# Two transformer blocks in one kernel: another order of block two's input chunks, later rotations in block one, one selection product, and one early Exp

## The reference, cut to what matters

```python
u = _rmsnorm(h, norm_mix)
p = _split_columns(u @ w_in)          # q_a k_a v_a | q_b k_b v_b q_idx k_idx w_idx | q_c k_cmp v_cmp k_sel v_sel k_win v_win g_c | g_merge
o_a = _stick_breaking(q_a, k_a, v_a)                    # log_sigmoid and exp of scores
o_b = _dsa_attention(_rope(q_b), rope1(k_b), v_b, _rope(q_idx), rope1(k_idx), w_idx)      # top 64 keys
o_c = _nsa_attention(_rope(q_c), rope1(k_cmp), v_cmp, rope1(k_sel), v_sel, rope1(k_win), v_win, gates, ...)
merged = g[0] * (o_a @ w_up[0]) + g[1] * (o_b @ w_up[1]) + g[2] * (o_c @ w_up[2])
```

## Time and profile before

| | us |
|---|---|
| median of 3 runs | 909.33 |
| lowest, highest of them | 908.6, 909.56 |
| the profiled execution, its own time | 909.91 |
| its span, first to last instruction | 907.4 |
| PE busy in the span | 882.2 |
| DVE, ACT, POOL busy | 606.8, 480.5, 29.2 |

### The profile page before, as it was taken

The page is one execution under the profiler, slowest core; times in us unless marked ns, Lnnn a source line. Parts: engine busy times, 40 slices in busy tenths (PEclk is TensorE's granted clock), DMA queues, the critical chain, the costliest instruction groups (busy, mean ns, idle before and its releaser), DMA issues.

```text
span 907.4 us, 15435 instructions
## 1 busy us (share of the span) xinstructions
PE 882.2 (97%) x6552; PEld 748.8 (83%) x6552; DVE 606.8 (67%) x976; ACT 480.5 (53%) x775; POOL 29.2 (3%) x51
## 2 busy tenths in 40 slices
PE   7999999999899999999999999999999999999997
PEld 4999898787689888888889978776788788888885
DVE  4578978557856666656766577877863566666673
ACT  4775667436534444456444856484622545555561
POOL 0010000010000000000000020000000000000000
PEclk9999999999999999999999999999999999999999
DMA  9644333224468665555339764353817566665521
GB/s 336 190 140 140 99 119 114 63 83 150 178 248 282 188 190 190 200 202 187 121 112 229 164 210 144 111 186 107 277 38 206 146 187 188 191 193 194 199 95 47
DMA packets 131204, 150.71 MB, mean 166 GB/s; under 512 B 11808, under 2 KB 102176, under 8 KB 131008
## 3 DMA queue, kind: packets, MB, share of 16 engines
q1 hardware_dynamic: 129920, 145.57, 51.8%
q10 hardware_dynamic: 1216, 4.16, 1.2%
HBM read 148.67 MB, written 1.05 MB: 165 GB/s over the span
## 4 chain that ended last, share of the span: by engine, by line
PE 85%; DVE 7%; ACT 4%; issue 2%; DMA 1%; POOL 0%; POOLq 0%; ACTq 0%; DVEq 0%
PE psum L821 12%; PE psum L716 9%; PE psum L718 9%; PE psum L717 9%; PE psum L826 7%; PE psum L774 4%; PE psum L794 3%; PE psum L795 3%; PE psum L803 3%; PE psum L722 3%; PE psum L870 2%; PE psum L880 2%; PE psum L871 2%; PE psum L827 2%; DVE parts L2705 2%
## 5 line engine op out<-in xcount | busy, mean ns | idle before, releaser
L1808 ACT ACTIVATE parts<-low 128x1024 fp32r<-128x1024 f32 (+3 forms) x252 | 254.3, 1044 | 65.6 <-PE psum L718 48.3
L2705 DVE TENSOR_TENSOR parts<-low,parts 128x1024 fp32r<-128x1024 f32 (+3 forms) x156 | 183.7, 1206 | 37.7 <-ACT parts L1808 37.5
L716 PE MATMUL psum<-parts 128*128 128x512 f32 (+2 forms) x424 | 169.1, 399 | 4.6 <-DVE parts L2705 2.5
L718 PE MATMUL psum<-parts 128*128 128x512 f32 (+2 forms) x424 | 163.5, 386 | 0.0
L717 PE MATMUL psum<-parts 128*128 128x512 f32 (+2 forms) x424 | 163.4, 385 | 0.0
L1808 ACT ACTIVATE high<-psum 128x512 f32<-128x512 f32 (+6 forms) x115 | 63.4, 560 | 134.2 <-PE psum L827 76.4
L821 PE MATMUL psum<-parts 128*128 128x512 f32 x462 | 116.8, 392 | 0.0
L716 PEld LDWEIGHTS psum<-parts 128*128 128x128 f32 x424 | 79.6, 188 | 26.3 <-DVE parts L2705 4.5
L821 PEld LDWEIGHTS psum<-parts 128*128 128x128 f32 x462 | 86.9, 188 | 16.9
L718 PEld LDWEIGHTS psum<-parts 128*128 128x128 f32 x424 | 79.6, 188 | 16.4
L717 PEld LDWEIGHTS psum<-parts 128*128 128x128 f32 x424 | 79.8, 188 | 13.9
(11 more groups left out here) (313 smaller groups left out, 1310.6 us busy)
## 6 DMA issues: line engine op xcount, KB each, us to landing
low<-in_w_in_dram SPq DMA_DIRECT2D x40, 1024.0 KB, 5.3
low<-in_w_ffn_in_dram SPq DMA_DIRECT2D x44, 512.0 KB, 5.2
low<-in_w_ff_in_dram SPq DMA_DIRECT2D x16, 1024.0 KB, 5.7
low<-in_w_ff_out_dram SPq DMA_DIRECT2D x16, 1024.0 KB, 4.8
low<-in_w_ffn_out_dram SPq DMA_DIRECT2D x11, 1024.0 KB, 5.0
low<-in_w_out_dram SPq DMA_DIRECT2D x8, 1024.0 KB, 5.2
low<-in_w_ple_gate_dram SPq DMA_DIRECT2D x4, 1024.0 KB, 5.0
low<-consts_dram ACTq DMA_DIRECT2D x1, 2078.0 KB, 9.0
```

The source lines that it names most:

```text
L716: mm(o, l[0], r[0], start, False)
L718: return mm(o, l[1], r[0], False, stop)
L1808: return e.activation(o, a, ACT.Copy)
L2705: tt(rslot3(n, nk, width)[:, r, 0:w], slot3(n, nk, width)[:, r, 0:w], st.hi3(j)[:, r, 0:w].bitcast(F32), ALU.subtract) \
```

## The change

It has five parts.

1. The order of `plan_2` is now: q_b, q_idx, the four keys, the narrow k_cmp with v_cmp, q_c. `rope_to` and the numbers in the waits follow. The function `ahead` goes, so every split stands in its place ahead of the wait for the chunk. The copies of keys on ACT move from the end of the last chunk into `read_vt`. The values' `token_range` uses banks 5 and 6.
2. Block one's rotations are done later (`turned_at`), with four buffers `rt1`.
3. The sum over four groups of partitions is one matmul for each head, against a new constant, `C_SEL`.
4. ACT does one Exp of one column after `main_b`.
5. The constants grow by 128 columns (from 2078 KB by 64 KB).

```diff
-C_END = C_SINC + 256
+C_SEL = C_SINC + 256
+C_END = C_SEL + 128
+    c[:, C_SEL:C_SEL + 16] = r % 32 == s[:, 0:16]
...
-        rt1 = [view3(P + 9216 + 1024 * i, 2, 256) for i in range(2)]
+        rt1 = [view3(P + 8704 + 512 * i, 2, 256) for i in range(4)]
...
-            return RC[:, 6:10:3, :] if n == 5 else RC[:, 10:11, :] if n == 6 else RC[:, 2 * (n - 2):2 * (n - 2) + 2, :]
+            return RC[:, 6:10:3, :] if n == 4 else RC[:, 10:11, :] if n == 5 else RC[:, 4:6, :] if n == 6 else RC[:, 2 * (n - 2):2 * (n - 2) + 2, :]
...
         plan_2 = [([(0, 256, 0)], [128, 128]), ([(256, 256, 0)], [128, 128]), ([(768, 256, 0)], [128, 128]),
-                  ([(1152, 256, 0)], [128, 128]), ([(1476, 256, 0)], [128, 128]),
-                  ([(1024, 64, 0), (1408, 64, 64), (1860, 64, 128), (1988, 64, 192)], [128, 128]), ([(1732, 128, 0)], [128])]
+                  ([(1152, 256, 0)], [128, 128]), ([(1024, 64, 0), (1408, 64, 64), (1860, 64, 128), (1988, 64, 192)], [128, 128]),
+                  ([(1732, 128, 0)], [128]), ([(1476, 256, 0)], [128, 128])]
...
-                yield from token_range(st2, 5, 2, 464, lambda i: [main_act.at("vt2", i), main_dve.at("vt2", i)], nothing)
+                yield from token_range(st2, 5, 2, 464, lambda i: [main_act.at("vt2", i), main_dve.at("vt2", i)], nothing, (5, 6))
...
-                    for g in range(4):
-                        t = mm(p[:, 16 * h:16 * h + 16], hd[:, h, :], ident[:, 32 * g:32 * g + 16], g == 0, g == 3)
+                    t = mm(p[:, 16 * h:16 * h + 16], hd[:, h, :], const(C_SEL, 16), True, True)
...
-            def ahead(st, j):
-                return st.tag == "st2" and j == 5
             def feature_chunk(st, j, widths, read):
                 steps = 1 + len(widths)
                 for n in range(steps):
-                    if n == 1 or n == 0 and not ahead(st, j + 1):
+                    if n < 2:
                         split(st, j + 1, (n,))
                     yield
                 q.wait_ge(*main_pe.at(st.tag, j, 1))
-                if ahead(st, j + 2):
-                    split(st, j + 2, (0,))
                 read()
...
-                if n >= (2 if tag == "qk" else 4):
-                    q.wait_ge(*rope_dve.at(tag, n - 2))
+                if n >= 4:
+                    q.wait_ge(*rope_dve.at(tag, n - (4 if tag == "qk" else 2)))
...
             def read_vt(i, p):
+                if i == 0:
+                    q.wait_ge(*rope_dve.at("in2", 4))
+                    for m, half in enumerate(half_rows[::-1]):
+                        copy(RC[half, 7, :], RC[half_rows[1], 6, :]).then_inc(key_act.up(m), 1)
+                    q.wait_ge(*key_act.at(1))
+                    copy(RC[half_rows[1], 6, :], RC[half_rows[0], 6, :]).then_inc(key_act.up(2), 1)
                 copy(vt[:, i, 0:256], p[:, 0:256])
...
             turns.alone(main_b())
+            act(first_exp, ident[:, 0:1], ACT.Exp).then_inc(stick_act.up("table"), 1)
...
+            turned_at = ((), (), (0,), (1,), (2, 3), (4,))
...
-                    yield from feature_chunk(st1, QK_AT + n, [128, 128], (lambda n=n: rope1(n - 1)) if n else nothing, nothing)
+                    yield from feature_chunk(st1, QK_AT + n, [128, 128], lambda n=n: [rope1(m) for m in turned_at[n]], nothing)
```

More of the change, by code:

```diff
@@ L351, in program @@
         sm_nsa = [(small(4), small(4), small(4), small(4)) for _ in range(2)]
+        first_exp = small(1)
         sm_mem = [(small(4), small(4), small(4)) for _ in range(2)]
@@ L833, in wide_chunk, with token_range @@
                 yield
-            def token_range(st, j0, n, w, freed, late):
+            def token_range(st, j0, n, w, freed, late, banks=None):
                 nk = 8 // n
-                banks = [next(pg), next(pg)]
+                banks = banks or [next(pg), next(pg)]
                 for s in range(n):
@@ L1541, in scores @@
                     bank(b)
-                q.wait_ge(*rope_dve.at("in2", 5))
+                q.wait_ge(*rope_dve.at("in2", 6))
                 q.wait_ge(*key_act.at(2))
@@ L1626, in nsa @@
                     bank(b)
-                q.wait_ge(*rope_dve.at("in2", 4))
+                q.wait_ge(*rope_dve.at("in2", 6))
                 q.wait_ge(*cmp_act.at("kc"))
@@ L1884, in feature_chunk, with token_range @@
                 q.wait_ge(*main_pe.at(st.tag, j, 1))
-                if ahead(st, j + 2):
-                    split(st, j + 2, (0,))
                 read()
                 yield
-            def token_range(st, j0, n, read):
+            def token_range(st, j0, n, read, banks=None):
                 nk = 8 // n
-                banks = [next(pg), next(pg)]
+                banks = banks or [next(pg), next(pg)]
                 for s in range(n):
@@ L1895, in token_range @@
                         for r in range(nk // 2):
-                            if i == 0 and (r == 1 or r == 0 and not ahead(st, j0 + s + 1)):
+                            if i == 0 and r < 2:
                                 split(st, j0 + s + 1, (r,))
@@ L2000, in qkv @@
                     b = next(pg)
-                    yield from feature_chunk(st1, QK_AT + n, [128, 128], lambda: rope_read("qk", n, 2, b, rt1[n % 2], qk[:, 2 * n:2 * n + 2, :]))
+                    yield from feature_chunk(st1, QK_AT + n, [128, 128], lambda: rope_read("qk", n, 2, b, rt1[n % 4], qk[:, 2 * n:2 * n + 2, :]))
             def gate(r):
@@ L2363, in read2 @@
                 else:
-                    m = 1 if n == 6 else 2
+                    m = 1 if n == 5 else 2
                     rope_read("in2", n, m, b, rz2[n % 2][:, 0:m, :], rope_to(n))
@@ L2376, in main_b @@
                     yield from feature_chunk(st2, n - 2, plan_2[n][1], lambda: read2(n, b))
[L2377 to L2383, removed]
+                yield from token_range(st2, 5, 2, read_vt, (5, 6))
             turns.alone(main_b())
+            act(first_exp, ident[:, 0:1], ACT.Exp).then_inc(stick_act.up("table"), 1)
             pa2 = itertools.cycle((2, 3, 4))
@@ L2742, in feature_chunk, with token_range @@
                 yield
-            def token_range(st, j0, n, read, late):
+            def token_range(st, j0, n, read, late, banks=None):
                 nk = 8 // n
-                banks = [next(pg), next(pg)]
+                banks = banks or [next(pg), next(pg)]
                 for s in range(n):
@@ L3291, in rope2 @@
                 if n >= 2:
-                    m = 1 if n == 6 else 2
-                    rope("in2", n, m, rz2[n % 2][:, 0:m, :], rope_to(n), *((C_COSC, C_SINC) if n == 6 else (C_COS, C_SIN)))
+                    m = 1 if n == 5 else 2
+                    rope("in2", n, m, rz2[n % 2][:, 0:m, :], rope_to(n), *((C_COSC, C_SINC) if n == 5 else (C_COS, C_SIN)))
             def read_vt(i, p):
                 if i == 0:
-                    q.wait_ge(*rope_dve.at("in2", 5))
+                    q.wait_ge(*rope_dve.at("in2", 4))
                     for m, half in enumerate(half_rows):
@@ L3310, in main_b @@
                     yield from feature_chunk(st2, n - 2, plan_2[n][1], lambda: rope2(n - 1), nothing)
-                yield from token_range(st2, 5, 2, read_vt, lambda: rope2(6))
+                yield from token_range(st2, 5, 2, read_vt, lambda: rope2(6), (5, 6))
             turns.alone(main_b())
@@ L3834, in nsa_keys @@
                 e.memset(blk[:, :, 15:32], 0.0).then_inc(cmp_pool.up("pad"), 1)
-                q.wait_ge(*rope_dve.at("in2", 6))
+                q.wait_ge(*rope_dve.at("in2", 5))
                 for n in range(15):
```

2 lines of the change are left out of this document (1 added, 1 removed).

## The result

| | before | after |
|---|---|---|
| median of 12 runs each, us | 909.56 | 911.4 |
| lowest to highest | 908.6 to 909.99 | 910.62 to 912.21 |
| profiled execution, its own time | 909.91 | 912.17 |
| its span | 907.4 | 910.2 |

The ratio after to before is 1.0023, 95% interval 1.0014 to 1.0031. The change makes the kernel slower by 0.23%, where 0.29% faster was forecast; 911.4 lies outside the range. The profiled execution of after is 0.8 us above its median and that of before 0.35, so the traces differ by a little more than the medians do.

A forecast was written before the change was run, and what follows sets the result against it. PE was taken as the bound, busy 882.2 of 907.4 us, so only its work and gaps count. Terms -1.2 - 0.4 + 0.3 - 1.3 = -2.6 us took 909.33 to 906.7 us, range 905.2 to 909.9.

The forecast's parts named there:

- the key chunk's landing: main_b: key chunk's four transfers taken to land at 502.7, costing +0.3 us, bounds 0 and +6.8.
- the later rotations: Block one: moving a rotation from ahead of the mask products removes PE's gaps of 1.04 and 0.16 us, -1.2 us.
- The stop before q_c: End of main_b: PE waits 2.65 us because q_c's split comes only after ACT reads the key chunk.
- those of the values: End of main_b: both old stops of the first values slot go; 0.8 us before the second slot.
- the -0.4 forecast: New order in main_b: 4.05 us lost to stops before, 3.65 us after, landing time counted separately.
- SP issues them within some 3 us: Key chunk in main_b: SP was to issue its four 256 KB transfers from 494.2 within some 3 us.
- the 4.1 I used: Key chunk's transfers: landing 4.1 us after issue in the median, taken from an empty queue at 499.1.
- The second rival: Key chunk waits in SP's backed-up queue behind w1; slower, 913.2 us for a landing at 509.2; 10%.
- The bounds: Block one's later rotations: the -1.2 us could lie between -1.2 and +0.7 us.
- Selection and Exp: Attention stage: PE arrives 1.43 us earlier, what it waits for 1.28 earlier, net -1.3 us; selection alone 0, Exp alone 0.41.
- The late landing: Rival in main_b: 256-byte rows at half rate land the key chunk at 504.5, stop 2.1 us, 908.5 us; 17%.

The follow-up runs named there:

- e2: The kernel before with the new order of main_b (part 1) alone: 913.64 us, ratio 1.0047.
- e8: The kernel before with the early Exp (part 4) alone: 907.95 us, ratio 0.9984.
- e10: The kernel before with the later rotations (part 2) alone: 908.96 us, ratio 0.9996.
- e7: The kernel before with the selection product (part 3) alone: 909.09 us, ratio 0.9999.
- e9: The changed kernel with four small matmuls, result not read, behind the last chunk of main_b: 910.69 us, ratio 1.0015.
- e11: e3 with 19 matmuls, result not read, where PE stood idle before q_c: 907.39 us, ratio 0.9978.
- e4: e3 with q_c's split on ACT ahead of reading the key chunk, and q_c's result in bank 7: 906.53 us, ratio 0.9967.
- e3: The changed kernel with the compression's weights loaded behind the key chunk instead of ahead of it: 910.12 us, ratio 1.0007.
- e6: e4 with the second values slot's split also ahead of reading q_c, plus four small unread matmuls before the attention stage: 904.44 us, ratio 0.9950.
- e12: The kernel before with the selection product and the early Exp (parts 3 and 4) together: 907.73 us, ratio 0.9981.

## Why the prediction was wrong, step by step

In short: one term of the sum was mis-sized (the key chunk's landing, +0.3 said, +1.8 found), and two costs were put at nothing, the slow clock behind a stop (+1.5) and a late packet of PE's instructions (+1.7). The other terms came out near their forecasts in the trace of after, save the later rotations, which brought less.

**The stop before q_c, and those of the values (part 1): right.** 2.67 for 2.65, 0.62 for 0.8, and both stops of the first slot gone. The order on ACT was as taken. From 504 to 536 the traces differ by +3.0 us; without the late landing (1.8) and the slow clock (1.5) that leaves -0.3, for the -0.4 forecast.

**When the key chunk lands (part 1): the term that was mis-sized.** +0.3 said, +1.8 in after. "SP issues them within some 3 us" failed: that came from an empty queue, and behind the compression's weights the last issue started 5.16 us after the first. The last piece then landed about 4.6 us after its issue, near the 4.1 I used. The short rows were slow as well, 199 GB/s against 349 with the engines full; how much of the lateness is theirs no run here separates, since a slower rate may also hold up the issuing. The Trainium skill, DMA: Bandwidth & Descriptors, section Specifications, wants transfers of at least 512 bytes for full rate; these rows are 256 bytes, and the trace agrees. I also set landing against PE's old arrival. PE came 0.7 us earlier, and that went into the stop as well: 0.92 in e2, 1.78 in after. The second rival put the break-even at a landing of 505.3; it came at 503.3, so this term alone does not make the kernel slower.

**The clock (nowhere in the prediction).** Every stop was priced at its length. It can cost more, in a part of the executions: PE's clock goes to the lower level for some 3 us behind it. That was 1.5 us in the profiled execution of after and 1.4 in e2's. It is less where a later stop takes it up: 0.4 in e8 and e10, and nothing in e7, where the stop of 1.49 us before the second slot of values went in return. In e9 the time goes with the clock, and in e11 and e4 the spread of e3 shrinks with the stop. How much of the median of after is the clock isn't shown. That falls come only behind stops rests on fourteen profiles with five falls, behind stops of 1.78 (after), 2.67 (e2), 1.23 and 0.64 (e7) and 1.88 and 1.81 us (e8, e10, in block one, where before has 1.75 and no fall); e3 and e9 have the stop of 2.67 and no fall. Why a stop is followed by a fall in one execution and not in the next stays open.

**The pause in the train (nowhere in the prediction).** +1.7. PE's next packet of instructions landed later, behind a burst of weights. e6 and e9 moved the program back by four matmuls and nothing else, and the pause went both times; e11 moved the packet at an unchanged time. So the packet is fetched by place in the program. Why the new order changed the place (it took a few waits out of PE's program) is my reading, and the number of places that matter was not measured.

**The later rotations (part 2): mechanism right, gain not.** -1.2 said, -0.9 in after, -0.35 alone (no change, by its interval). The gap went, and in e10 gaps marked "issue" took most of its place; in after the key chunk's stop took what was left. Of the 0.9, 0.3 is luck: the stop at 230 us is 1.45 in after and 1.75 in before, and e2, with the old rotations, has 1.43. The bounds allowed for a smaller gain, the value taken did not.

**Selection and Exp (parts 3 and 4): right together, wrong in how they share.** -1.3 said, -1.6 in e12, -1.3 in its trace and in that of after. The selection alone gives 0, as said; the Exp alone gives 1.2, not 0.4, and so all of it. On the table load the measured rows decide: the load at 560.55 ends at 561.83, and the Ln stands at 561.85 in after. The Trainium skill, ScalarE: Activation LUTs, section What ACT_TABLE_LOAD costs, has a drain of 1.380 us beside the load of 1.283; the load agrees, and there is no room for the drain.

**The rivals.** The late landing (17%) came true in its size, near the 2.1 us it gave, with its slower rate and with the slow issuing of the second (10%) beside it. Neither made the time: a sum that holds all that the prediction named, with the late landing, is about 908.2 (909.33 - 2.6 + 1.5), and the trace of after has the 3.2 us from there to 911.4 in the clock (1.5) and the packet of instructions (1.7). The range left out that two costs unseen in the trace of before could come together.

## What to carry to other kernels

Look at the granted clock behind a stop of PE, and allow for more than its length unless another stop follows that can take it up. Fill it or move the split ahead of the read (e4), and compare the lowest execution as well as the median. Price transfers by their issue in the queue as it stands there, and set their landing against the arrival that the rest of the change gives. When a pause has no releaser ("issue"), look for the instruction queue among the DMA queues, and try a few instructions more or less before the place. Take the gain of a stage from a point where the traces are alike to the end: a gap alone gave 1.36 us for a pause that cost 1.7, and 0.4 for an Exp that brought 1.3.

## What the runs showed of the hardware

- A granted clock of 0.51 for 3 us behind a stop of 1.78 us, with PE busy throughout; one program ran between 908.96 and 912.91 us as its mean clock lay between 0.999 and 0.994.
- The same slow stretch cost 1.5 us in after, 0.4 in e10 and nothing in e7, where a stop of 1.49 us behind it went.
- 19 matmuls in an idle stop (2.4 us) brought the spread of executions from 3.2 us to 1.0.
- A packet of PE's instructions behind a burst that held the DMA engines at a share of 1.00 left a pause of 1.3 to 1.6 us (1.36, 1.42, 1.29, 1.60 and 1.30 in five kernels), ending 1.29 to 1.38 us after the packet had landed, and made a train of 2.03 us last 3.7 to 4.0; four matmuls of 32x16 ahead of it took the pause away.
- Four transfers of 256 KB took SP 6.74 us to issue behind 2 MB of weights. With the DMA engines full, rows of 256 bytes moved at 199 GB/s and rows of 1 KB at 349.
